# PEER query projection as three fp32r products of high and low halves, with the halves written by the last norm's eviction

## The chip, the cores and the metric

The kernel runs on one core of one Trainium2 chip. The metric is the device time of one execution in microseconds. TensorE is called PE here, VectorE the DVE, ScalarE ACT, GpSimd POOL and the queue that issues most loads SP.

## The reference, cut to what matters

Two transformer blocks run over 512 tokens (four tiles of 128) of width 1024. The change is in the last part of the second block, a layer of experts chosen by product keys (PEER):

```
h2 = rms_norm(x, norm2_g) * (1 + scale2) + shift2
qp = (h @ w_pq).reshape(b, s, 8 heads, 2, 128)          # w_pq is 1024 x 2048
sc = einsum("bshpd,hpnd->bshpn", qp, sub_keys)           # 128 scores for each head and half
s1, i1 = top_k(sc[..., 0, :], 16); s2, i2 = top_k(sc[..., 1, :], 16)
top_s, top_c = top_k(s1[..., :, None] + s2[..., None, :], 16)
expert = e1 * 128 + e2; gate = softmax(top_s)
y = sum over heads and picks of gate * gelu(u[expert] . h) * v[expert]
x = x + gate2 * y
```

## The kernel before

Everything is float32. Large products are done in one of two ways. A plain float32 matmul takes its operands as they are, and shows in the trace as two matmul records. A split product uses fp32r operands: an operand is rounded to a high half, the low half is what is left, and three matmuls (high x high, low x high, high x low, in `passes`) are summed in PSUM.

**Weights** come in 70 chunks of 128 x 2048 through a ring of six buffers. SP loads chunk c once the count `w_used` says that chunk c - 6 is used. The output projection of the second block has chunks 58 to 61, the queries have chunks 62 to 69 (`W_PQ` = 62), each for two of the 16 query blocks. For split chunks the high half is a copy to fp32r by ACT (`high_part`, L693), the low half a subtraction, by the DVE (`low_part`, L1175) or by POOL (`split`, L543 and L545). Before, the query chunks aren't split.

**Output projection and norm.** `mixed_linear` on PE goes over four tiles of tokens and four chunks (L1902). The DVE adds each result to x (L1506, L1509). ACT forms the root mean square of a tile (L626, L629) once that tile's x is complete, the DVE scales the tile (L1060), PE transposes it (L1796), and the DVE's `evac` (L1074, L1076) multiplies by the gain and adds the shift, writing the transposed, normalised tile to hT. On ACT this order is `mix_and_norm`, in which the norm of the last tile comes last.

**Queries and scores.** `queries(c, lo, hi)` (L2131) multiplies block c of w_pq by hT. Blocks 0 and 1 are done on the first three tiles (384 columns) and, when the last tile is through the norm, on its 128 columns. Then h2 of the last tile is transposed back (L2146), and for c = 2 to 16 PE does query block c (512 columns) and the scores of block c - 1 (L2164). ACT copies queries (L959) and scores (L962) out of PSUM.

**Best keys.** For each head the DVE finds the 16 best keys of each half and the 16 best pairs for tiles 0, 1 and 2: `key_tops` and `pair_tops` (L1528 to L1556), 24 units, each head's behind the scores of its two blocks. Between the last units it forms ranks and picks of tile 0 (`tile_ranks`, `tile_keys`, L1573 to L1589). Then 96 chunks of one-hot tables follow (L1645, L1649), which PE multiplies (L2258) into gate tables that are written to memory.

**Experts.** For three tiles all 16384 experts are computed densely; the fourth tile gathers its rows. PE starts with `half_in(s)`, half a key's 128 experts: transposes of u (L2182), the low half of u by a product with the negative identity (L2204), and the split product with h (hd_hi, hd_lo; L2196). 16 of these halves come before the one-hot chunks, the others at fixed places among them. The order is written out by hand on each engine: PE transposes tile 0's picks (`slot_transposes(0)`, L2236) after half 10; ACT takes the exponential of the gates of tile 0 (L981) after half 4, when unit 23 of the DVE is done, and of tiles 1 and 2 after half 14. After 1543 us PE's main loop over 128 keys runs (L2196, L2223).

hd_hi and hd_lo, the halves of h for three tiles, are made by the DVE from hT after the last `evac` (L1517, L1519).

Of the kernel before, what the change touches and what calls it, by code (L numbers as in the profile page):

```python
# [7 lines left out]
ALU = mybir.AluOpType  # L8
# [71 lines left out]
def build(nc, wst, wada, x_in, meta_in, cols_in, rowsa_in, rowsb_in, rope_in, const_in, pos_in,  # L80
          subk_in, peer_u, peer_v, out):
    ctx = ExitStack()
    with ctx:
# [149 lines left out]
        gtmp = cut(r1, 10240, 2, 256)  # L233
        keys = cut(r1, 10720, NKEYS)

        r1_at = big_at + 4 * (WR * CH + 4224 + 17312)
        hd_hi = cut(halves("hd_hi", r1_at + 4 * 4096, KD * DN), 0, KD, DN)
        hd_lo = cut(halves("hd_lo", r1_at + 4 * (4096 + KD * DN), KD * DN), 0, KD, DN)
# [18 lines left out]
        slotT = [gates[:, 0, 0:384], gates[:, 0, 384:768], r1[:, 10240:10624]]  # L257
# [5 lines left out]
        topf = cut(r1, 11104, 2, SLOTS)  # L263
        picks = [v.rearrange("p (a s) -> p a s", a=2) for v in (gates[:, 0, 768:1024], r1[:, 10848:11104], rowsb[:, 0:256])]
# [96 lines left out]
        def high_of(c):  # L361

            if c < W_GU:
                return (mid_hi if c < W_OUT + 2 else w2_hi)[:, (c - W_OUT) % 2, :]
            if c == W_IN2 + 2:
                return w3_hi
            if c < W_LAT:
                return (w_hi if c < W_IN2 else w2_hi)[:, (c - W_GU) % 2, :]
            return (w2_hi if c < W_O2 + 2 else o2_hi)[:, (c - W_O2) % 2, :]
# [161 lines left out]
        def _(pool):  # L531
# [44 lines left out]

            pool.wait_ge(w_used, W_PQ)
            pool.dma_start(subk, subk_in).then_inc(subk_in_s, 16)

# [21 lines left out]
        def _(act):  # L601
# [83 lines left out]
            def high_part(c):  # L685

                chunk(act, c)
                if W_IN2 <= c < W_IN2 + 3:
                    act.wait_ge(a_lo_done, 6)
                    act.wait_ge(w_used, W_IN2 - 2)  # L690
                elif W_GU + 2 <= c < W_LAT:
                    act.wait_ge(w_used, c - 1)
                act.activation(high_of(c), ring[:, c % WR, :], ACT.Copy).then_inc(w_hi_done, 1)  # L693
# [220 lines left out]
            mix_and_norm(T, 3, xn4)  # L914

# [50 lines left out]
            def slots_evac(t):  # L966
                act.wait_ge(slot_tr, t + 1)
                act.activation(slotT[t], ps[:, 2, 0:384], ACT.Copy).then_inc(slot_ready, 1)
# [77 lines left out]
        def _(v):  # L1046
# [4 lines left out]
            def norm(layer, tiles, buf):  # L1051
# [10 lines left out]
                def evac(t):  # L1062
# [9 lines left out]
                    if layer == 3:  # L1072
                        shift = mod[:, 24:24 + KD]
# [502 lines left out]
            def tile_ranks(t):  # L1576

                v.tensor_copy(topf.rearrange("p a s -> p (a s)"), topi[:, t, :])
                pair_ranks(besti[:, t, :], rank_bits, ranks, wrap)
# [59 lines left out]
            for t in range(DT):  # L1639
                v.wait_ge(slot_ready, t + 1)  # L1640
                for c in range(NCH):
# [3 lines left out]
                    v.tensor_tensor(one[n % 4][0], each(keys, CHUNK), over(slotT[t][:, CHUNK * c:CHUNK * c + CHUNK], NKEYS),  # L1645
                                    ALU.is_equal)
                    for k in range(CHUNK):
                        at = CHUNK * c + k
                        mk = v.tensor_scalar(one[n % 4][1][:, k, :], keys, slotT[t][:, P + at:P + at + 1],  # L1649
                                             slotT[t][:, 2 * P + at:2 * P + at + 1], ALU.is_equal, ALU.mult)  # L1650
# [129 lines left out]
        def _(pe):  # L1780
# [364 lines left out]
            for k in range(KD):  # L2145
                mm = pe.transpose(ps[:, 4 + k // 4, P * (k % 4):P * (k % 4) + P], hT[:, k, DT * P:T * P], ident)  # L2146
# [94 lines left out]
            pe.wait_ge(hd_ready, DT)  # L2241
# [118 lines left out]
```

## Time and profile before

| what | value |
|---|---|
| median of 3 runs | 2610.83 us (2608.54 to 2611.42) |
| profiled execution | 2610.15 us, of which the span is 2608.3 us |
| PE busy | 2490.9 us (95%) |
| DVE busy | 1744.4 us (67%) |
| ACT busy | 961.4 us (37%) |
| POOL busy | 376.3 us (14%) |
| mean granted PE clock | 0.989 |

All times of rows are microseconds from the start of the span, mean durations of one instruction are in ns where a row says so. Busy shares are averages over stages with different limits, so that they don't tell what one stage waits for; the views of single stretches do. Matmuls are pipelined: the step from one start to the next is their price, not the length of one record.

### The profile page before, as it was taken

To read this page: it belongs to the slowest core of one execution; us is meant where nothing else is said; L and a number is where in the kernel's file an instruction comes from. 1 tells how busy PE (TensorE), PEld (TensorE's weight loads), DVE (VectorE), ACT (ScalarE), POOL (GpSimd) and SP (SyncE) were. 2 spreads that over 40 slices of the span, in tenths; PEclk is the share of its full clock that TensorE was granted. 3 is DMA by queue.
4 is the path that set the end of the run, shared out by engine and by line. 5 is a ranking of instruction groups with operands and counts; after the bars stand their busy time and mean duration, and the time that the engine had idled before them with its cause. 6 is when DMAs were issued, how large, how long until landed. Compare 5 with 4: busy or idle time off the path is not lost.

```text
span 2608.3 us, 37914 instructions
## 1 busy us (share of the span) xinstructions
PE 2490.9 (95%) x13765; PEld 2137.5 (82%) x13765; DVE 1744.4 (67%) x3801; ACT 961.4 (37%) x1723; POOL 376.3 (14%) x353
## 2 busy tenths in 40 slices
PE   8998889999998989999989999999999999999998
PEld 6777778777778957784688989899899989999987
DVE  5526556553235565548899977887878787877765
ACT  4325532222232645511255653333333333333332
POOL 1000210110000000100000002333333333332300
PEclk9999999999999999999999999999999999999999
DMA  4110005662221220022024567888878887887764
GB/s 187 65 49 1 1 33 192 222 238 99 81 97 66 81 81 1 1 98 73 25 65 170 194 254 275 290 286 284 276 268 282 288 279 268 290 285 259 261 195 153
DMA packets 123511, 431.43 MB, mean 165 GB/s; under 512 B 11696, under 2 KB 36528, under 8 KB 111168
## 3 DMA queue, kind: packets, MB, share of 16 engines
q1 hardware_dynamic: 74768, 241.20, 26.7%
q0 software_dynamic: 47520, 186.14, 20.3%
q8 instruction: 112, 1.84, 0.3%
q10 hardware_dynamic: 1040, 1.67, 0.2%
q14 instruction: 71, 0.58, 0.1%
HBM read 399.61 MB, written 29.36 MB: 164 GB/s over the span
## 4 chain that ended last, share of the span: by engine, by line
PE 75%; DVE 16%; ACT 3%; issue 2%; DVEq 2%; ACTq 1%; DMA 0%
PE ps L2223 19%; PE ps L2196 16%; PE ps L1949 10%; PE ps L1902 7%; PE ps L1806 5%; PE ps L1988 5%; DVE r L1649 4%; PE ps L2182 3%; DVE r L1645 2%; PE ps L2121 1%; PE ps L1871 1%; PE ps L1844 1%; PE ps L2066 1%; ACT r L700 1%; PE ps L2131 1%
## 5 line engine op out<-in xcount | busy, mean ns | idle before, releaser
L2196 PE MATMUL ps<-hd_hi,uT_hi 128*128 128x384 f32 x1024 | 349.9, 342 | 0.8 <-ACT uT_lo L951 0.7
L2196 PE MATMUL ps<-hd_hi,uT_lo 128*128 128x384 f32 x1024 | 346.5, 338 | 0.0
L2196 PE MATMUL ps<-hd_lo,uT_hi 128*128 128x384 f32 x1024 | 346.3, 338 | 0.0
L2223 PE MATMUL ps<-v_hi,ew_hi 128*128 128x512 f32 x768 | 319.5, 416 | 3.7 <-DVE ew_lo L1622 3.1
L2223 PE MATMUL ps<-v_hi,ew_lo 128*128 128x512 f32 x768 | 303.5, 395 | 0.0
L2223 PE MATMUL ps<-v_lo,ew_hi 128*128 128x512 f32 x768 | 301.4, 392 | 0.0
L1602 DVE TENSOR_TENSOR uT_lo<-ps,uT_hi 128x512 fp32r<-128x512 f32 x204 | 140.8, 690 | 144.8 <-ACT uT_hi L924 144.7
L924 ACT ACTIVATE uT_hi<-ps 128x512 fp32r<-128x512 f32 x256 | 152.2, 595 | 189.8 <-PE ps L2182 189.7
L2196 PEld LDWEIGHTS ps<-hd_hi,uT_lo 128*128 128x128 f32 x1024 | 192.6, 188 | 11.0
L2196 PEld LDWEIGHTS ps<-hd_hi,uT_hi 128*128 128x128 f32 x1024 | 192.7, 188 | 9.6 <-ACT uT_lo L951 1.3
L596 POOL DMA_INDIRECT big<-peer_u,r x128 | 144.1, 1126 | 335.3 <-DVE r L1706 311.9
L2196 PEld LDWEIGHTS ps<-hd_lo,uT_hi 128*128 128x128 f32 x1024 | 192.5, 188 | 0.0
L596 POOL DMA_INDIRECT big<-peer_v,r x128 | 143.0, 1117 | 336.3 <-DVE big L1716 326.6
L1607 DVE TENSOR_TENSOR v_lo<-r,v_hi 128x1024 fp32r<-128x1024 f32 x128 | 156.9, 1225 | 38.6 <-ACT v_hi L931 38.6
L1716 DVE SCALAR_TENSOR_TENSOR big<-big,r 128x1024 f32<-128x1024 f32 x128 | 164.5, 1285 | 14.8 <-DMA big<-peer_v,r 2.5
L2223 PEld LDWEIGHTS ps<-v_hi,ew_lo 128*128 128x128 f32 x768 | 144.4, 188 | 32.8
L2223 PEld LDWEIGHTS ps<-v_hi,ew_hi 128*128 128x128 f32 x768 | 144.7, 188 | 29.9 <-DVE v_lo L1607 5.9
L2223 PEld LDWEIGHTS ps<-v_lo,ew_hi 128*128 128x128 f32 x768 | 145.3, 189 | 25.0
L1175 DVE TENSOR_TENSOR w_lo<-big,w_hi 128x2048 fp32r<-128x2048 f32 x42 | 96.0, 2291 | 102.5 <-ACT w_hi L693 102.5
L1706 DVE CUSTOM_DVE_ANT_0 big<-big,r 128x1024 f32<-128x1024 f32 x128 | 155.6, 1218 | 4.0 <-DMA big<-peer_u,r 4.0
L2182 PE MATMUL ps<-const,r 128*128 128x128 f32 x1024 | 153.2, 272 | 3.2 <-DVE uT_lo L1602 3.2
L1806 PE MATMUL ps<-big 128*128 128x256 f32 (+1 forms) x656 | 149.7, 383 | 0.3 <-issue 0.3
(351 smaller groups left out, 5228.5 us busy)
## 6 DMA issues: line engine op xcount, KB each, us to landing
big<-wst SPq DMA_DIRECT2D x70, 1024.0 KB, 4.9
r<-peer_u SPq DMA_DIRECT2D x128, 512.0 KB, 6.9
r<-peer_v SPq DMA_DIRECT2D x128, 512.0 KB, 4.8
r<-wada POOLq DMA_DIRECT2D x48, 512.0 KB, 4.7
gd<-big POOLq DMA_DIRECT2D x24, 1024.0 KB, 8.1
big<-gd SPq DMA_DIRECT2D x32, 768.0 KB, 9.6
x<-x_in SPq DMA_DIRECT2D x4, 512.0 KB, 6.5
xd<-x SPq DMA_DIRECT2D x4, 512.0 KB, 10.2
```

Of the source, the lines that this page charges most:

```text
L596: pool.indirect_dma_start(rows[n % RW], None, table, bass.IndirectOffsetOnAxis(ap=idx[:, n:n + 1], axis=0)).then_inc(got[n % RW], 16)
L924: act.activation(uT_hi[:, s % 2], ps[:, in_bank(s), :].rearrange("p (k n) -> p k n", k=KD // 2), ACT.Copy).then_inc(u_hi_done, 1)
L1602: v.tensor_tensor(uT_lo[:, s % 2], ps[:, in_bank(s), :].rearrange("p (k n) -> p k n", k=KD // 2), uT_hi[:, s % 2].bitcast(F32), ALU.subtra ...
L1607: v.tensor_tensor(v_lo[:, i % VR, :], vraw[:, i % VR, :], v_hi[:, i % 2, :].bitcast(F32), ALU.subtract).then_inc(v_lo_done, 1)
L1706: v.tensor_tensor_reduce(out=urows[n % RW], in0=urows[n % RW], in1=h2, scale=1.0, scalar=0.0, op0=ALU.mult, op1=ALU.add, accum_out=dots[:, ...
L1716: v.scalar_tensor_tensor(out=yacc[:, n % 2, :], in0=vrows[n % RW], scalar=wts[:, n:n + 1], in1=yacc[:, n % 2, :], op0=ALU.mult, op1=ALU.ad ...
L1806: mm = pe.matmul(ps[0:r, bank, 0:w], hT[:, k, t * P:t * P + r], wt[:, k, 0:w], start=(k == 0), stop=(k == KD - 1))
L1902: mm = pe.matmul(ps[:, bank, 0:256], h[:, k, t * P:(t + 1) * P], w[:, k, :], start=(k == 0 and i == 0), stop=(k == KD - 1 and i == 2))
L1949: mm = pe.matmul(ps[:, 2 * (f % 2) + u, lo:hi], w[:, k, u, :], h[:, k, lo:hi], start=(k == 0 and i == 0), stop=(k == KD - 1 and i == 2))
L2182: mm = pe.matmul(ps[:, in_bank(s), P * k:P * k + P], uraw[:, j % UR, at:at + P], ident, is_transpose=True, start=(k == 0 or alone), stop=( ...
L2196: mm = pe.matmul(ps[:, acc_bank(j), 0:DN], w[:, k, :], h[:, KD // 2 * half + k, :], start=(half == 0 and k == 0 and i == 0), stop=(half == ...
L2223: mm = pe.matmul(ps[:, 2 + 2 * t + half, :], w[:, P * t:P * t + P], vv[:, 512 * half:512 * half + 512], start=(i == 0 and n == 0), stop=(i ...
```

## The change

- The four query operands are halves now: w_pq is split, with the high half written by ACT (`high_part`, into two buffers `pq_hi`) and the low half by POOL (`query_low`, into `w_lo`). `queries` does three fp32r matmuls for each of the eight blocks of 128 in place of one float32 matmul. It waits for `w_lo_done`, not for the chunk's load.
- ACT does `high_part` of chunks 62 and 63 after `mix_and_norm`, of 64 to 69 in the loop of the query and score copies, one after every second block.
- POOL issues the load of the sub-keys after the low halves of chunks 62 and 63, and before it did so as its first act in this part.
- `evac` of the last norm writes the sum to a tile of its own (`hq_full`, `h3_full` for the last tile), and then the high half `hq_hi` and the low half `hq_lo`, all on the DVE. The DVE's later split of hT into hd_hi and hd_lo is gone: hd_hi is a part of hq_hi, and hd_lo is a copy of hq_lo that ACT makes at c = 13, when chunk 68 is used.
- Some small tiles move into gaps of hq_hi's buffer (keys, slotT, picks, topf).

```diff
+        hq_hi = cut(halves("hq_hi", r1_at + 4 * 4096, KD * 512), 0, KD, 512)
+        hd_hi = hq_hi[:, :, 0:DN]
+        gaps = cut(r1, 4096, KD, 512)[:, :, DN:512]
+        hq_lo = h_hi[:, :, 0:512]
...
+            def query_low(c):
+
+                if c == W_PQ:
+                    pool.wait_ge(w_lo_done, split_no(W_PQ - 1))
+                pool.wait_ge(w_hi_done, split_no(c))
+                pool.tensor_tensor(w_lo[:, c % WR, :], ring[:, c % WR, :], high_of(c).bitcast(F32),
+                                   ALU.subtract).then_inc(w_lo_done, 1)
+
+            query_low(W_PQ)
+            query_low(W_PQ + 1)
             pool.wait_ge(w_used, W_PQ)
             pool.dma_start(subk, subk_in).then_inc(subk_in_s, 16)
+            for c in range(W_PQ + 2, NCHUNK):
+                query_low(c)
...
-                elif W_GU + 2 <= c < W_LAT:
+                elif W_GU + 2 <= c < W_LAT or c >= W_PQ + 2:
                     act.wait_ge(w_used, c - 1)
+                elif c == W_PQ + 1:
+                    act.wait_ge(mixt_tr, 2 * T)
...
             mix_and_norm(T, 3, xn4)
+            high_part(W_PQ)
+            high_part(W_PQ + 1)
...
+                if c % 2 and W_PQ + c // 2 + 2 < NCHUNK:
+                    high_part(W_PQ + c // 2 + 2)
+                if c == 13:
+                    act.wait_ge(w_used, NCHUNK - 1)
+                    act.wait_ge(ln_hT, 17)
+                    act.activation(hd_lo, hq_lo[:, :, 0:DN], ACT.Copy).then_inc(hd_ready, 1)
...
-                        v.tensor_tensor(dst, src, over(g, n), ALU.mult)
+                        full, high = h3_full if t == T - 1 else hq_full, hq_hi[:, :, at]
+                        v.tensor_tensor(full, src, over(g, n), ALU.mult)
                         v.drain()
-                        v.tensor_tensor(dst, dst, over(shift, n), ALU.add).then_inc(ln_hT, 1)
+                        v.tensor_tensor(full, full, over(shift, n), ALU.add)
+                        v.drain()
+                        v.tensor_copy(high, full)
+                        v.drain()
+                        v.tensor_tensor(hq_lo[:, :, at], full, high.bitcast(F32), ALU.subtract).then_inc(ln_hT, 1)
+                        v.drain()
                         return
...
-            for t in range(DT):
-                full = hT[:, :, t * P:t * P + P]
-                v.tensor_copy(hd_hi[:, :, t * P:t * P + P], full)
-                v.drain()
-                v.tensor_tensor(hd_lo[:, :, t * P:t * P + P], full, hd_hi[:, :, t * P:t * P + P].bitcast(F32),
-                                ALU.subtract).then_inc(hd_ready, 1)
...
-                wt = ring[:, (W_PQ + c // 2) % WR, :].rearrange("p (k n) -> p k n", k=KD)
+                chunk_no = W_PQ + c // 2
+                w_parts = [w.rearrange("p (k n) -> p k n", k=KD)[:, :, P * (c % 2):P * (c % 2) + P]
+                           for w in (high_of(chunk_no), w_lo[:, chunk_no % WR, :])]
                 for k in range(KD):
-                    mm = pe.matmul(ps[:, c % 4, lo:hi], wt[:, k, P * (c % 2):P * (c % 2) + P], hT[:, k, lo:hi],
-                                   start=(k == 0), stop=(k == KD - 1))
+                    for i, (w, h) in enumerate(passes(w_parts, (hq_hi, hq_lo))):
+                        mm = pe.matmul(ps[:, c % 4, lo:hi], w[:, k, :], h[:, k, lo:hi],
+                                       start=(k == 0 and i == 0), stop=(k == KD - 1 and i == 2))
                 return mm
 
-            chunk(pe, W_PQ)
+            pe.wait_ge(w_lo_done, split_no(W_PQ))
             pe.wait_ge(ln_hT, 16)
             queries(0, 0, DN)
...
-                    chunk(pe, W_PQ + c // 2)
+                    pe.wait_ge(w_lo_done, split_no(W_PQ + c // 2))
...
-            pe.wait_ge(hd_ready, DT)
+            pe.wait_ge(hd_ready, 1)
```

## Rows read from the trace of the kernel before

**Rows 1.** Windows, whole core: length, busy time by engine, granted clock, DMA.
```profile
1343.00:1520.00 177.00, 167.16 (x1216) 162.70 (x1215) 175.72 (x496) 95.54 (x164) 11.15 (x20) 0.97 0.43 161
1543.00:2608.00 1065.00, 1054.84 (x5560) 944.83 (x5559) 801.58 (x1266) 369.29 (x587) 283.94 (x253) 1.00 0.77 264
```
**Rows 2.** Waits of the DVE, 1150 to 1600: total, times, longest.
```profile
DVE r L1528 <- ACT r L962: 12.9, 1, 12.9
```
**Rows 3.** Chain that ended last, 1168 to 1186.
```profile
1170.26 6.87 PE ps L2131 x16
1177.12 0.91 PE ps L2164 x8
...
1178.68 0.29 DVE r L1528
```
**Rows 4.** Timeline of the DVE: units 1, 2 and 23.
```profile
1181.86 0.28 DVE L1545 TENSOR_TENSOR r<-r 128x120 f32<-128x120 f32 x1
...
1184.08 0.48 DVE L1528 MAX8 r<-r 128x8 f32<-128x128 f32 x2
...
1303.49 0.22 DVE L1556 TENSOR_SCALAR r<-r 128x16 f32<-128x16 f32 x1
```
**Rows 5.** Timeline of PE around the last norm.
```profile
1151.28 5.40 PE L2131 MATMUL ps<-big 128*128 128x384 f32 x16 [0.26 <-issue]
1156.51 1.04 PE L1796 MATMUL ps<-const,r 128*128 128x128 f32 x8
...
1166.39 1.09 PE L2146 MATMUL ps<-const,big 128*128 128x128 f32 x8
```
**Rows 6.** Timeline of ACT: end of the last norm.
```profile
1153.33 0.29 ACT L629 ACTIVATE lnst<-lnst,eps 128x1 f32<-128x1 f32 x1
```
**Rows 7.** Weight splits by source line: duration ns min/median/max.
```profile
L693 ACT ACTIVATE w_hi<-big x42: 1897/1908/1917, 382.1 to 902.9; 128x2048 fp32r<-128x2048 f32 x42
```
```profile
L545 POOL TENSOR_TENSOR w_lo<-big,w_hi x4: 4517/4524/4532, 320.5 to 1082.5; 128x2048 fp32r<-128x2048 f32 x4
```
**Rows 8.** Timeline of PE: 47 fp32r matmuls of 128 columns, 47 of 512.
```profile
415.56 0.28 PE L1949 MATMUL ps<-h_hi,w_lo 128*128 128x128 f32 x1
...
420.70 0.27 PE L1949 MATMUL ps<-h_lo,w_hi 128*128 128x128 f32 x1
...
432.98 0.39 PE L1949 MATMUL ps<-h_hi,w_lo 128*128 128x512 f32 x1
...
443.60 0.40 PE L1949 MATMUL ps<-h_lo,w_hi 128*128 128x512 f32 x1
```
**Rows 9.** Timeline of the DVE: last eviction and split of h.
```profile
1157.59 1.23 DVE L1074 TENSOR_TENSOR big<-ps,gs 128x1024 f32<-128x1024 f32 x1 [2.94 <-PE ps L1796]
...
1160.03 0.69 DVE L1517 CAST hd_hi<-big 128x1024 fp32r<-128x1024 f32 x1
1160.79 1.23 DVE L1519 TENSOR_TENSOR hd_lo<-big,hd_hi 128x1024 fp32r<-128x1024 f32 x1
```
**Rows 10.** DVE L1202 by source line, and a timeline beside POOL.
```profile
L1202 DVE SCALAR_TENSOR_TENSOR r<-r,coef x16: 767/769/3165, 201.2 to 341.1; 128x528 f32<-128x528 f32 x16
```
```profile
327.37 4.52 POOL L545 TENSOR_TENSOR w_lo<-big,w_hi 128x2048 fp32r<-128x2048 f32 x1
...
329.28 3.17 DVE L1202 SCALAR_TENSOR_TENSOR r<-r,coef 128x528 f32<-128x528 f32 x1
```
**Rows 11.** PE's first matmul after a wait, and the window around it.
```profile
805.65 0.39 PE L1902 MATMUL ps<-w_hi,h_hi 128*128 128x256 f32 x1 [3.87 <-DVE h_lo L1088]
```
```profile
805.00:810.00 5.00, 4.35 (x24) 4.38 (x24) 0.66 0.01 3
```
**Rows 12.** DMA issues, 1100 to 1200: KB each, us to landing.
```profile
r<-subk_in POOLq DMA_DIRECT2D x1, 1024.0 KB, 8.4
```
**Rows 13.** Chain that ended last, 1318 to 1345: halves, then ACT.
```profile
1321.23 1.06 PE ps L2196 x6
...
1333.01 1.28 ACT L981
```

More of the change, by code:

```diff
@@ L232, in build @@
         xn4 = cut(r2, 14336, 2, D)
-        gtmp = cut(r1, 10240, 2, 256)
-        keys = cut(r1, 10720, NKEYS)
+        gtmp = cut(r2, 16384, 2, 256)
         r1_at = big_at + 4 * (WR * CH + 4224 + 17312)
-        hd_hi = cut(halves("hd_hi", r1_at + 4 * 4096, KD * DN), 0, KD, DN)
-        hd_lo = cut(halves("hd_lo", r1_at + 4 * (4096 + KD * DN), KD * DN), 0, KD, DN)
+        hq_hi = cut(halves("hq_hi", r1_at + 4 * 4096, KD * 512), 0, KD, 512)
+        hd_hi = hq_hi[:, :, 0:DN]
+        hd_lo = cut(halves("hd_lo", r1_at + 4 * 8192, KD * DN), 0, KD, DN)
+        gaps = cut(r1, 4096, KD, 512)[:, :, DN:512]
+        keys = gaps[:, 3, :]
+        hq_lo = h_hi[:, :, 0:512]
+        hq_full = cut(r1, 10240, KD, P)
+        h3_full = cut(gates[:, 0, :], 0, KD, P)
+        pq_hi = [cut(halves("pq_hi0", r1_at + 4 * 8192, CH), 0, CH), cut(halves("pq_hi1", r2_at + 4 * 12288, CH), 0, CH)]
         uraw = cut(r2, 9216, UR, D)
@@ L256, in build @@
         one = [[cut(r1, CHUNK * P * (2 * b + a), CHUNK, P) for a in range(2)] for b in range(4)]
-        slotT = [gates[:, 0, 0:384], gates[:, 0, 384:768], r1[:, 10240:10624]]
+        slotT = [cut(gates[:, 0, :], 0, 3, P), cut(gates[:, 0, :], 384, 3, P), gaps[:, 0:3, :]]
         xback = [cut(big, 8192 + D * i, D) for i in range(T)]
@@ L262, in build @@
         wrap = rowsa[:, 0:SLOTS]
-        topf = cut(r1, 11104, 2, SLOTS)
-        picks = [v.rearrange("p (a s) -> p a s", a=2) for v in (gates[:, 0, 768:1024], r1[:, 10848:11104], rowsb[:, 0:256])]
+        topf = gaps[:, 6:8, :]
+        picks = [cut(gates[:, 0, :], 768, 2, P), gaps[:, 4:6, :], cut(rowsb, 0, 2, P)]
         gring = cut(big, 0, 2, 2 * DT, GB * HT)
@@ L366, in high_of @@
                 return w3_hi
+            if c >= W_PQ:
+                return pq_hi[(c - W_PQ) % 2]
             if c < W_LAT:
@@ L964, in _ @@
                                    ACT.Copy).then_inc(sk_ev, 1)
+                if c % 2 and W_PQ + c // 2 + 2 < NCHUNK:
[4 more added lines that the diff above has]
+                    act.activation(hd_lo, hq_lo[:, :, 0:DN], ACT.Copy).then_inc(hd_ready, 1)
             def slots_evac(t):
                 act.wait_ge(slot_tr, t + 1)
-                act.activation(slotT[t], ps[:, 2, 0:384], ACT.Copy).then_inc(slot_ready, 1)
+                act.activation(slotT[t], ps[:, 2, 0:384].rearrange("p (k n) -> p k n", k=3), ACT.Copy).then_inc(slot_ready, 1)
             def half_evac(s):
@@ L1072, in evac @@
                     if layer == 3:
-                        shift = mod[:, 24:24 + KD]
-                        v.tensor_tensor(dst, src, over(g, n), ALU.mult)
+                        shift, at = mod[:, 24:24 + KD], slice(t * P, (t + 1) * P)
+                        full, high = h3_full if t == T - 1 else hq_full, hq_hi[:, :, at]
+                        v.tensor_tensor(full, src, over(g, n), ALU.mult)
                         v.drain()
-                        v.tensor_tensor(dst, dst, over(shift, n), ALU.add).then_inc(ln_hT, 1)
+                        v.tensor_tensor(full, full, over(shift, n), ALU.add)
[4 more added lines that the diff above has]
+                        v.drain()
                         return
@@ L1576, in tile_ranks @@
             def tile_ranks(t):
-                v.tensor_copy(topf.rearrange("p a s -> p (a s)"), topi[:, t, :])
+                v.tensor_copy(topf, topi[:, t, :].rearrange("p (a s) -> p a s", a=2))
                 pair_ranks(besti[:, t, :], rank_bits, ranks, wrap)
@@ L1644, in _ @@
                         v.wait_ge(g_acc, n - 3)
-                    v.tensor_tensor(one[n % 4][0], each(keys, CHUNK), over(slotT[t][:, CHUNK * c:CHUNK * c + CHUNK], NKEYS),
+                    v.tensor_tensor(one[n % 4][0], each(keys, CHUNK), over(slotT[t][:, 0, CHUNK * c:CHUNK * c + CHUNK], NKEYS),
                                     ALU.is_equal)
@@ L1648, in _ @@
                         at = CHUNK * c + k
-                        mk = v.tensor_scalar(one[n % 4][1][:, k, :], keys, slotT[t][:, P + at:P + at + 1],
-                                             slotT[t][:, 2 * P + at:2 * P + at + 1], ALU.is_equal, ALU.mult)
+                        mk = v.tensor_scalar(one[n % 4][1][:, k, :], keys, slotT[t][:, 1, at:at + 1],
+                                             slotT[t][:, 2, at:at + 1], ALU.is_equal, ALU.mult)
                     mk.then_inc(one_ready, 1)
@@ L2145, in _ @@
             for k in range(KD):
-                mm = pe.transpose(ps[:, 4 + k // 4, P * (k % 4):P * (k % 4) + P], hT[:, k, DT * P:T * P], ident)
+                mm = pe.transpose(ps[:, 4 + k // 4, P * (k % 4):P * (k % 4) + P], h3_full[:, k, :], ident)
             mm.then_inc(h2_tr, 1)
```

## Prediction

> **What bounds the kernel now.** I read the windows of busy time first. In 1343 to 1520 us the DVE is busy 175.72 of 177 us, while PE still has gaps; from 1543 us to the end PE is busy 1054.84 of 1065 us [rows 1]. So the end of the run is set by PE from 1543 us on, and the moment at which that last part begins is set by something before it. The waits of the DVE over 1150 to 1600 us say by what: one long wait, 12.9 us, for the second score eviction (ACT L962), and after it only short ones [rows 2]. The chain of waits confirms it: third query product, score product, DVE at 1178.68 [rows 3], and from there DVE instructions one behind another. The DVE does one unit (key_tops and pair_tops of one tile and one head) in 1184.08 - 1178.68 = 5.40 us, and the 23rd ends at 1303.7 us [rows 4], with no wait for PE among them. A head is three units, 16.2 us, and on PE two query products and two score products: 2 x (6.87 + 0.91) = 15.6 us [rows 3] and some 0.5 us for drains, just less. Then come the DVE's ranks and one-hot tables to 1543 us. The reader should see that between 1179 and 1543 us PE's time costs nothing by itself; the start of the DVE's first unit and whatever stops the DVE count one for one.
>
> **What the change does to the start of the first unit.** Before, query product 0 starts at 1151.28 us, right behind the output projection [rows 5]. Now it waits for the low half of weight chunk 62. That is POOL's subtraction behind ACT's rounded copy, and in ACT's order the copy stands behind the norm of tile 3, whose last instruction ends at 1153.33 + 0.29 = 1153.62 us [rows 6]. The copy takes 1.91 us and POOL's subtraction 4.52 [rows 7]: 1153.62 + 1.91 + 4.52 + 0.05 = 1160.1 us. Late by **8.8 us**. The two other conditions of that product are met earlier: the eviction of tile 2 grows by a cast and a subtraction, 0.76 + 1.23 = 2 us [rows 9], but it lies inside the projection of tile 3, where the DVE waits for PE; without that idle time each of its 2 us would count.
>
> Prices of the new products, from rows of the same shape: 512 columns, 46 steps in 443.60 - 432.98 us, 0.231 us each, so 24 take 5.54; 128 columns, 46 steps in 420.70 - 415.56, 0.112 each [rows 8]; 384 columns, six in 1.06 us, 0.176 each, so 24 take 4.2 [rows 13].
>
> Query 0 on three tiles took 1156.51 - 1151.28 = 5.23 us; now 4.2 at full clock. But PE has stood 9 us. After a wait of 3.87 us at 805.65 us the granted clock was 0.66 over the next 5 us, that is 1.2 GHz for about 3.4 us and then 2.4 [rows 11]; 3.4 us at the lower level give back half, 1.5 to 1.7. Net **+0.5**.
>
> From the transposes of tile 3 (1156.51) to those of h2 (1166.39) were 9.88 us [rows 5]. Now the eviction starts 1.08 us after the first transpose (1157.59 against 1156.51) and is a product, a sum, a cast and a subtraction: 2.44 + 0.10 for a drain + 0.76 + 1.23 = 4.5 us [rows 9], so it ends 5.6 us after the first transpose, when PE is done with query 1 (0.9 + 4.2) and has waited half a us. Then the last tile's share of queries 0 and 1, 48 products at 0.112: 5.4 us. Together 11.1, **+1.2**. (At 128 columns three passes cost more than the old two.) From the h2 transposes to query 2 nothing changes. Query 2 itself: 5.54 for 6.87, **-1.3**.
>
> The sub-key load, which POOL now issues behind two subtractions (near 1164.7 us), lands in 8.4 us [rows 12], by 1173.2; PE asks for it at about 1178. Hidden by 5 us; each us beyond that would count. The loads of weight chunks follow the used counts and are early too. The first unit starts 8.8 + 0.5 + 1.2 - 1.3 = **9.2 us** later, near 1187.9 us.
>
> **What is gained and not seen.** Thirteen further query products save 1.33 us each, 17 us of PE. PE then needs about 13.4 us a head (2 x (5.54 + 0.91) + 0.5) where the DVE needs 16.2, and it reaches the expert part 17.3 - 9.2 = 8 us earlier than before, at about 1186 + 13 x 6.7 + 2 = 1275. There it runs until ACT stops at the gate exponential of tile 0, which waits for the DVE's 23rd unit. The DVE loses the split of hd (six instructions, 5.8 us), but it did these before 1166 us, right ahead of its long wait [rows 2, 9]: worth nothing. ACT's six further copies of 1.91 us and the 3072-element copy of the low halves (about 2.8 us by the length of the 2048-element one) lie between its copies: per query block of at least 5.5 us it has only two short ones to do.
>
> **What POOL does to the DVE.** Six more subtractions of 4.52 us run on POOL (chunks 64 to 69). The first ends about when unit 1 starts; five fall into the units. Each unit has, 3.18 us from its start, a tensor_tensor with both inputs in SBUF (L1545) [rows 4]. The nearest row is the attention's scalar_tensor_tensor (L1202), also with two SBUF inputs: 0.77 us alone, but 3.17 us when it started inside a POOL subtraction, ending at 332.45, 0.56 us after POOL's end at 331.89 [rows 10]. The DVE stood until POOL was through. So a POOL subtraction that covers L1545 stops the DVE for its remainder. POOL follows the query pace of 13.4 us: after release the DVE passes one L1545 at 5.40, before the next subtraction begins (13.4 - 4.5 = 8.9), and meets it with the next at 10.8, 1.9 us into it: 2.6 us lost, and the pattern repeats itself. Only the first of the five, whose phase is open, can cost anything between 0 and 4.5. I take 2.5 for each of the five, **12.6 us**, by the row of L1202. Bounds: 0 (L1545 isn't held) and 5 x 4.52 = 22.6. Between them lies a shared port that only slows both: L1202 grew to 3.17 / 0.77, four times its length; four times 0.28 us is 0.85 us more, five times, 4 us. Against that stands that L1202 ended so close behind POOL.
>
> The Trainium skill, "SBUF — State Buffer", section "SBUF: two separate sides", calls what the two engines share "an exclusive lock, not a bandwidth split", held for a whole instruction by the one that starts first. By that rule the term is 12.6 us, by a split it would be the 4; the trace agrees with the rule where it can be seen, L1202 ending 0.56 us behind POOL's 4.52 us instruction.
>
> **The restart.** A half takes (1333.0 - 1321.2) / 4 = 2.9 us [rows 13]. PE does six by about 1293 and then stands until unit 23 ends, at 1303.7 + 9.2 + 12.6 = 1325.5: some 30 us, and its clock falls as in [rows 11]. The halves behind it run at 1.2 GHz for 3.4 us, and the chain from the slot transposes to the exponentials of tiles 1 and 2 runs through PE (the halves, then ACT at 1333.01) [rows 13]. Part of the 1.7 us lies in waits for ACT: I take **0.5 us**, bounds 0 and 1.7.
>
> **Sum.** 9.2 + 12.6 + 0.5 = 22.3 us on the DVE's chain. What follows is shifted as a whole, since PE's halves are at fixed places among the one-hot chunks. The profiled execution took 2610.15 us (span 2608.3 and 1.85 around it), which makes 2632.5; the median is 0.7 us higher. I say **2633 us**.
>
> **Rivals.**
> 1. POOL doesn't hold the DVE, or by a split only: 2610.8 + 9.7 = 2620.5, with the split 2625. For it: L1545 is short, 120 elements, and no row shows such a one beside POOL. Against it: L1202. Chance 0.17.
> 2. Every subtraction costs the DVE nearly its whole length, because more of the unit's instructions are held or the phases fall badly, and the restart costs 1.7: 9.2 + 22.6 + 1.7 = 33.5, 2644. The unit's other instructions have one input in SBUF or a few elements, which speaks against. Chance 0.12.
> 3. Faster: the DVE's units follow the scores, and PE's gain reaches the end: 9.2 - 17.3 = -8.1, 2603. It takes a unit under 13.4 / 3 = 4.5 us; it is 5.40 [rows 4]. Chance 0.04.
> 4. No effect: the low half of chunk 62 is ready in time and POOL harmless. ACT's order forbids it. Chance 0.03.
>
> My forecast has 0.64: its own range is 2626 to 2640. The range of 8 in 10 takes in rival 1's lower value and reaches towards rival 2: 2619 to 2641. About 5 us (0.2%) is what measurement tells from no change. Faster 0.04, same 0.03, slower 0.93.
>
> **What would show it.** PE should stand about 9 us before the first query product, waiting for POOL's w_lo, with a fall of the granted clock behind it. DVE L1528 should first start at 1187 to 1189. Query products should take 5.5 us, PE should stand some 30 us in the expert part's halves. L1545 should show a maximum of 2 to 5 us, five or so times, each ending with a POOL subtraction; if all are 0.28, rival 1 holds. I'd be wrong in kind if the first DVE unit started before 1180, or if the units waited for scores.

## The result and the profile after

| | before | after |
|---|---|---|
| median of 4 runs, us | 2610.24 | 2635.7 |
| lowest and highest, us | 2608.54 to 2611.42 | 2632.94 to 2637.85 |
| profiled execution, us | 2610.15 | 2632.94 |
| span, us | 2608.3 | 2631.1 |
| mean granted clock | 0.989 | 0.982 |

The changed kernel is slower: the ratio is 1.0097, with an interval of 1.0085 to 1.0109, or 25.5 us between the medians.

The windows of busy time, in the columns of [rows 1], show the same two parts as before, both 23 us later. Windows of the same lengths hold nearly the same instructions and busy times as in [rows 1], so nearly the whole difference was made ahead of 1366 us.

```profile
1366.00:1543.00 177.00, 165.05 (x1217) 159.92 (x1216) 175.74 (x495) 95.17 (x163) 11.29 (x20) 0.99 0.43 161
1566.00:2631.00 1065.00, 1055.91 (x5560) 946.10 (x5560) 801.98 (x1267) 369.91 (x589) 285.63 (x253) 1.00 0.77 264
```

Two waits of PE between 1145 and 1560 us (total, times, longest) are new: one for POOL's low half in front of the first query product, and one for ACT in the expert part's halves, where before PE waited 0.7 us for the same tile.

```profile
PE ps L2229 <- ACT uT_lo L975: 32.6, 2, 32.0
...
PE ps L2164 <- POOL w_lo L590: 9.1, 1, 9.1
```

How the first of them comes about is seen in the timelines of ACT, POOL and PE. The lines answer to [rows 5, 6, 7].

```profile
1151.67 0.30 ACT L649 ACTIVATE lnst<-lnst,eps 128x1 f32<-128x1 f32 x1
1151.87 3.69 ACT L715 ACTIVATE pq_hi<-big 128x2048 fp32r<-128x2048 f32 x2
```
```profile
1153.91 9.01 POOL L590 TENSOR_TENSOR w_lo<-big,pq_hi 128x2048 fp32r<-128x2048 f32 x2 [68.54 <-ACT pq_hi L715]
```
```profile
1149.08 0.28 PE L1932 MATMUL ps<-h_lo,mid 128*128 128x256 f32 x1
1158.47 0.69 PE L2164 MATMUL ps<-hq_hi,pq_hi 128*128 128x384 f32 x1 [9.10 <-POOL w_lo L590]
...
1164.54 1.03 PE L1826 MATMUL ps<-const,r 128*128 128x128 f32 x8
```

The projection's last product starts at 1149.08 us; ACT is through with the norm only at 1151.97, the first copy and the first subtraction (4.51 of the 9.01 us) follow, and the product starts at 1158.47. Moments of one trace can't be set against those of another here: already before the change's first instruction this trace runs 1.66 us ahead of the one of before, whose last product of the projection starts at 1150.74. So I compare lengths inside each trace, by this chain of waits, which answers to [rows 3]:

```profile
1158.47 6.23 PE ps L2164 x24
...
1170.26 5.58 PE ps L2164 x48
1175.83 0.11 issue
1175.94 1.10 PE ps L2179 x8
...
1179.81 5.51 PE ps L2164 x24
...
1186.88 0.29 DVE r L1558
```

From the projection's last product to the first instruction of the DVE's first unit it is 1186.88 - 1149.08 = 37.80 us, where before it was 1178.68 - 1150.74 = 27.94: 9.9 us more.

In the units, some DVE records are unusually long. Here is one beside POOL, in the timelines:

```profile
1209.01 4.61 POOL L590 TENSOR_TENSOR w_lo<-big,pq_hi 128x2048 fp32r<-128x2048 f32 x1 [8.78 <-ACT pq_hi L715]
```
```profile
1209.08 0.30 DVE L1578 MAX8 r<-r 128x8 f32<-128x136 f32 x1
1209.45 0.09 DVE L1580 MATCH_VALUE_LOAD r<-r 128x8 f32 x1
1209.53 0.29 DVE L1580 FIND_INDEX8 r<-r 128x8 uint32<-128x136 f32 x1
1209.74 0.07 DVE L1581 MATCH_VALUE_LOAD r<-r 128x8 f32 x1
1209.80 0.28 DVE L1581 MATCH_REPLACE8 r<-r 128x136 f32<-128x136 f32 x1
...
1210.82 2.83 DVE L1586 TENSOR_SCALAR r<-r 128x16 f32<-128x16 f32 x1
```

Eight DVE instructions, five of which are shown, run inside POOL's at their usual length. Then the TENSOR_SCALAR over 16 elements a partition takes 2.83 us in place of 0.22, and ends at 1213.65, with POOL's end at 1213.62. Five records of the units are so long: L1586 at 1197.55 (2.70), 1210.82 (2.83) and 1224.22 (2.76), L1574 at 1235.67 (4.68) and 1250.90 (2.75). Beyond the usual 0.22 that is 14.6 us. By source line (duration ns min/median/max), over the whole run:

```profile
L1574 DVE TENSOR_SCALAR r<-r x32: 227/234/4681, 1189.9 to 2243.9; 128x16 f32<-128x16 f32 x32
```
```profile
L1575 DVE TENSOR_TENSOR r<-r x32: 271/276/278, 1190.1 to 2244.0; 128x120 f32<-128x120 f32 x32
```

L1575 is the tensor_tensor with two SBUF inputs, the L1545 of [rows 4]. It was never held here.

The 23 units run from 1186.88 to the gate exponential of tile 0 at 1326.50: 139.6 us, where before it was 1303.83 - 1178.68 = 125.15. From there to the slot transposes of tile 0 it is 17.73 us, before 16.85, by these rows of PE and ACT, first of after, then of before:

```profile
1344.23 0.38 PE L2269 MATMUL ps<-const,gates 128*128 128x128 f32 x2
```
```profile
1326.50 0.40 ACT L1011 ACTIVATE r<-r,zero 128x128 f32<-128x128 f32 x1 [31.87 <-DVE r L1586]
```
```profile
1320.68 0.44 PE L2236 MATMUL ps<-const,gates 128*128 128x128 f32 x2 [0.42 <-DVEq L1589]
```
```profile
1303.83 0.40 ACT L981 ACTIVATE r<-r,zero 128x128 f32<-128x128 f32 x1
```

The three lengths add up to 9.9 + 14.5 + 0.9 = 25.2 us, beside 25.5 between the medians. The profiled executions differ by 22.8: the one of after is the lowest of its four, ran 1.66 us ahead in the part that the change doesn't touch, and took 0.75 us less from the slot transposes to the end (1286.87 for 1287.62).

### The profile page after: what moved, and what is told of

The parts are those of the page before. It is cut to its first block, busy times and chain, and to the rows that moved or that the text cites. A ratio compares the mean times of both kernels' runs of the same rounds, so it can differ in the third digit from the quotient of the medians.

```text
span 2631.1 us, 38239 instructions
## 1 busy us (share of the span) xinstructions
PE 2475.1 (94%) x13909; PEld 2165.0 (82%) x13909; DVE 1760.9 (67%) x3803; ACT 977.8 (37%) x1732; POOL 414.5 (16%) x361
## 4 chain that ended last, share of the span: by engine, by line
PE 75%; DVE 16%; ACT 3%; issue 2%; DVEq 2%; ACTq 1%; DMA 0%; POOL 0%; POOLq 0%
PE ps L2256 19%; PE ps L2229 16%; PE ps L1979 10%; PE ps L1932 7%; PE ps L1836 5%; PE ps L2018 5%; DVE r L1679 4%; PE ps L2215 3%; DVE r L1675 2%; PE ps L2151 2%; PE ps L1901 1%; PE ps L1874 1%; PE ps L2096 1%; ACT r L722 1%; DVE r L1238 1%
## 5 line engine op out<-in xcount | busy, mean ns | idle before, releaser
L2229 PE MATMUL ps<-hq_hi,uT_hi 128*128 128x384 f32 x1024 | 350.9, 343 | 32.6 <-ACT uT_lo L975 32.6
L2229 PE MATMUL ps<-hq_hi,uT_lo 128*128 128x384 f32 x1024 | 347.5, 339 | 0.0
L2229 PEld LDWEIGHTS ps<-hq_hi,uT_hi 128*128 128x128 f32 x1024 | 193.5, 189 | 41.4 <-ACT uT_lo L975 33.2
L2229 PEld LDWEIGHTS ps<-hq_hi,uT_lo 128*128 128x128 f32 x1024 | 193.3, 189 | 11.0
L1932 PE MATMUL ps<-w_lo,h_hi 128*128 128x256 f32 x528 | 148.8, 282 | 0.0
```

Source lines behind the costliest of these rows:

```text
L1932: mm = pe.matmul(ps[:, bank, 0:256], h[:, k, t * P:(t + 1) * P], w[:, k, :], start=(k == 0 and i == 0), stop=(k == KD - 1 and i == 2))
L2229: mm = pe.matmul(ps[:, acc_bank(j), 0:DN], w[:, k, :], h[:, KD // 2 * half + k, :], start=(half == 0 and k == 0 and i == 0), stop=(half == ...
```

## The experiments

All were timed beside the kernel before, whose median was 2610.65, 2610.2 and 2611.15 us beside the three groups of them (e1 to e4; e5, e6, e7, e9; e8 and e10). Gains are counted from the changed kernel's 2635.7 us. Three lengths are read from each trace, of which there is one a kernel: **start** (the projection's last product to the first MAX8 of the units), **units** (from there to the first gate exponential) and **slots** (from there to the first slot transpose).

| kernel | median, us | ratio to before, interval | start | units | slots |
|---|---|---|---|---|---|
| before | | | 27.94 | 125.15 | 16.85 |
| after | 2635.7 | 1.0097 [1.0085, 1.0109] | 37.80 | 139.62 | 17.73 |
| e1_no_low | 2618.54 | 1.0031 [1.0019, 1.0042] | 38.13 | 125.00 | 16.95 |
| e2_early | 2629.8 | 1.0071 [1.0057, 1.0085] | 27.18 | 139.63 | 17.85 |
| e3_pieces | 2625.43 | 1.0050 [1.0036, 1.0064] | 38.71 | 128.77 | 16.94 |
| e4_early_pieces | 2618.32 | 1.0031 [1.0022, 1.0041] | 28.80 | 128.72 | 16.98 |
| e5_dve_low | 2634.31 | 1.0086 [1.0072, 1.0099] | 38.68 | 136.23 | 18.20 |
| e6_swap | 2634.26 (one run) | | 37.94 | 139.82 | 17.74 |
| e7_warm | 2634.49 | 1.0093 [1.0078, 1.0107] | 37.80 | 139.67 | 17.67 |
| e8_all_pieces | 2613.89 | 1.0015 [1.0006, 1.0024] | 27.17 | 128.82 | 17.44 |
| e9_all | 2613.23 | 1.0010 [1.0001, 1.0019] | 27.20 | 128.74 | 16.93 |
| e10_two_chunks | 2609.34 | 0.9999 [0.9989, 1.0008] | 27.21 | 125.04 | 16.94 |

**e1_no_low: is it POOL's work that stretches the units?** The low halves of chunks 64 to 69 are left out; the second product of these takes the high half again.

```
-                query_low(c)
+                pool.wait_ge(w_hi_done, split_no(c))
+                pool.drain().then_inc(w_lo_done, 1)
...
-                           for w in (high_of(chunk_no), w_lo[:, chunk_no % WR, :])]
+                           for w in (high_of(chunk_no), w_lo[:, chunk_no % WR, :] if c < 4 else high_of(chunk_no))]
```

> The low halves of weight chunks 64 to 69 are left out: POOL forms none, and the second of the three query products takes the high half again, so that PE does as many products as in the changed kernel. Everything else is as changed. If POOL's subtractions hold the DVE's units (the trace of the changed kernel shows five TENSOR_SCALARs of 2.70, 2.83, 2.76, 4.68 and 2.75 us in place of 0.22), they fall to 0.22 and 14.6 us go: 2635.7 - 14.6 = 2621, or 10 to 11 us above the kernel before. Rival: the long records are only how the trace books a wait that the DVE would have anyway (for scores, or for PE); then the DVE waits elsewhere and the time stays at 2633 to 2637. Third: the whole loss is the late start; then also no change.

The units went back to 125.0 us, and no record of these lines is long, as by source line for L1575 of this kernel (its TENSOR_SCALAR over 16 elements):

```profile
L1575 DVE TENSOR_SCALAR r<-r x32: 225/234/288, 1190.2 to 2228.4; 128x16 f32<-128x16 f32 x32
```

17.2 us of the medians are gone, with as many PE products and the same ACT copies; 14.6 were expected. In the traces the units give back 14.6 us and the slots 0.8, and the profiled executions differ by 15.6; the rest of the 17.2 is no more than the runs of one kernel differ by. So the stretch of the units is POOL's, whole.

**e2_early: the other half, the late low half of chunk 62.** ACT copies the high halves of chunks 62 and 63 ahead of the norm of tile 2's sums, so that POOL makes the low halves during the projection.

```
+                    if t == T - 1 and first:
+                        high_part(W_PQ)
+                        high_part(W_PQ + 1)
...
-            high_part(W_PQ)
-            high_part(W_PQ + 1)
```

> The high halves of chunks 62 and 63 are made by ACT before the norms of tiles 2 and 3, so that POOL has both low halves when the output projection ends. The first query product should start within 0.5 us of its end, without a fall of the clock, and the DVE's first unit comes 9.9 us earlier than in the changed kernel, perhaps one more, since three passes over 384 and 512 columns are shorter. If the late start costs one for one, the time is 2635.7 - 10 to 11 = 2625 to 2626. Rival: POOL's two subtractions now lie beside the DVE's residual sums and evictions and hold them, so that PE waits in the projection instead; then up to 9 us of it come back and the time stays above 2630.

The first query product no longer waits, the start is 10.6 us shorter, but the median fell by 5.9 us only, where 10 to 11 were expected. The rest was lost again ahead of the start, in the norm of tile 2. Timelines of POOL, DVE and PE:

```profile
1130.57 9.35 POOL L590 TENSOR_TENSOR w_lo<-big,pq_hi 128x2048 fp32r<-128x2048 f32 x2 [42.48 <-ACT pq_hi L715]
```
```profile
1132.18 3.29 DVE L1546 TENSOR_TENSOR x<-x,r 128x256 f32<-128x256 f32 x1
1135.38 1.21 DVE L1106 TENSOR_TENSOR r<-ps,gs 128x1024 f32<-128x1024 f32 x1
1136.67 4.33 DVE L1108 TENSOR_TENSOR r<-r,mod 128x1024 f32<-128x1024 f32 x1
```
```profile
1147.64 1.97 PE L1827 MATMUL ps<-const,r 128*128 128x128 f32 x8 [3.20 <-DVE r L1091]
```

Two DVE instructions with both inputs in SBUF were held by the two subtractions (3.29 for 0.42 us and 4.33 for 1.23); the one between them, which reads a PSUM input, was not, though POOL was at work: 1.21. The norm's result came late, PE waited 3.2 us and went on at the lower clock (0.50 from 1147.6 to 1152 us): from the transposes to the projection's last product it is 1157.19 - 1147.64 = 9.55 us, in the changed kernel 1149.08 - 1142.08 = 7.0. That is 3.2 + 2.55 = 5.75 us lost for 10.6 won, 4.9 by these lengths beside 5.9 between the medians, and explains why not 10 us were gained. In the units one of the five long records now lies on the tensor_tensor with two SBUF inputs (at 1233.28, 4.69 us).

**e3_pieces: does the DVE wait for one POOL instruction, or for POOL's work?** The subtractions of chunks 64 to 69 are cut into eight instructions of 256 columns.

```
+                for j in range(8 if c >= W_PQ + 2 else 1):
+                    n = CH // 8 if c >= W_PQ + 2 else CH
+                    at = slice(n * j, n * j + n)
+                    low = pool.tensor_tensor(w_lo[:, c % WR, at], ring[:, c % WR, at], high_of(c)[:, at].bitcast(F32),
+                                             ALU.subtract)
+                low.then_inc(w_lo_done, 1)
```

> POOL's subtractions of chunks 64 to 69 are done in eight instructions of 256 columns each, the same elements in all. If POOL holds the DVE for the length of one instruction, a hold is at most some 0.7 us in place of 2.7 to 4.7; there may be two or three short ones where there was one long one, 1 us for each of five chunks: 14.6 falls to about 5 and the time to 2626. If instead what counts is the data that POOL moves (a shared bandwidth, the same elements), nothing changes: 2633 to 2637.

POOL now works longer, 5.60 us a chunk for 4.60, and yet the DVE loses 3.6 us in place of 14.5. Had POOL's busy time been what counts, it would have lost more. In the timelines of POOL and DVE:

```profile
1202.57 5.59 POOL L593 TENSOR_TENSOR w_lo<-big,pq_hi 128x256 fp32r<-128x256 f32 x8 [7.73 <-ACT pq_hi L719]
```
```profile
1207.66 0.53 DVE L1578 TENSOR_SCALAR r<-r 128x16 f32<-128x16 f32 x1
```

There are nine held instructions now in place of five. They take 0.53 to 0.88 us, never more than one piece (5.6 / 8 = 0.7 us) beyond their own length. What holds the DVE is the one POOL instruction in progress, for its remainder.

**e4_early_pieces: do the two parts add?** Both edits together.

> Both edits together: early high halves of chunks 62 and 63, and subtractions in eight pieces. If the two costs are independent terms of one chain, the gains add: 2635.7 - 10.5 - 9.6 = 2615.6, 5 us above the kernel before, of which about 5 are the short holds and 1 the colder restart. If both edits remove the same wait, it stays near 2625.

The gains are 5.9 and 10.3 us alone and 17.4 together: they add within the intervals. The 3.24 us wait for tile 2's norm is still there, since chunks 62 and 63 were not cut.

**e5_dve_low: the DVE makes the low halves itself.** One subtraction ahead of each of heads 0 to 5; POOL keeps chunks 62 and 63.

```
-            for c in range(W_PQ + 2, NCHUNK):
-                query_low(c)
...
+                if h == 0:
+                    v.wait_ge(w_lo_done, split_no(W_PQ + 1))
+                if W_PQ + h + 2 < NCHUNK:
+                    low_part(W_PQ + h + 2)
```

> The low halves of chunks 64 to 69 are made by the DVE itself, one ahead of each of heads 0 to 5, and POOL keeps only chunks 62 and 63. If the 14.6 us are POOL holding the DVE, no long record of L1574 or L1586 is left, and in their place stand six subtractions of 2.3 to 2.5 us on the DVE: 14 to 15 us, so the time stays at 2634 to 2636 us. Rival, that the units are longer for another reason (the eviction's new layout, ACT's writes): the long records stay and the six subtractions come on top, 2649 to 2651 us.

No record of the units is held, and the six subtractions take 2.29 us each, the first in the DVE's wait for the scores, five in the units, which are 11.1 us longer than before (14 to 15 were expected, with all six counted). The start and the slots are 0.9 and 0.5 us longer than in the changed kernel. The DVE's own work for these halves costs nearly what waiting for POOL's costs: 2634.31.

**e6_swap: which instruction is held?** In pair_tops the tensor_tensor of 128x120 comes ahead of the tensor_scalar of 128x16.

```
-                v.tensor_scalar(c0[:, 0:16], topv[:, 1, :], topv[:, 0, 0:1], None, ALU.add)
...
+                v.tensor_scalar(c0[:, 0:16], topv[:, 1, :], topv[:, 0, 0:1], None, ALU.add)
```

> In pair_tops the two instructions that build the candidates change places: first the tensor_tensor of 128x120, then the tensor_scalar of 128x16. Theory: POOL's instruction stops the first DVE instruction of a kind that can be stopped, whichever it is, while MAX8, FIND_INDEX8 and MATCH_REPLACE8 pass. Then at least one long record moves to the tensor_tensor with two SBUF inputs, the total beyond the normal lengths stays between 12 and 17 us, and the time stays within 3 us of 2635.7. Rival: only the tensor_scalar is stopped; then the tensor_tensor never exceeds 0.3 us and all long records stay on the two tensor_scalar lines.

There are five long records again, 14.7 us beyond the usual lengths. One of them has moved to the tensor_tensor (at 1252.84, 3.01 us); at 1237.90 the tensor_scalar behind it took 4.58. So both forms are held, and the one that comes first while POOL is at work is held.

**e7_warm: is the 0.9 us of the slots the clock's?** 280 transposes into a bank that nothing reads stand ahead of half 6.

```
+                if s == 6:
+                    for n in range(280):
+                        pe.transpose(ps[:, 5, 0:P], ident, ident)
```

> 280 transposes of 128x128 into a bank that nothing reads stand ahead of half 6, where PE stands 32 us in the changed kernel. Theory: the lower clock behind the wait costs the chain from the 23rd unit to the slot transposes 0.9 us; with PE busy this stretch is 17.0 us long in place of 17.9 and the time 2634.8 us, unless the transposes outlast the wait, which would show as a later half 6 and be longer by what they overrun. Rival: the clock's share lies in waits for ACT, and the stretch stays at 17.9.

The slots stayed at 17.67 us. The windows of this kernel show why (busy PE, PEld, DVE, ACT, POOL, granted clock, DMA):

```profile
1290.00:1327.00 37.00, 36.17 (x315) 35.77 (x313) 32.63 (x184) 3.56 (x7) 0.00 (x0) 1.00 0.10 30
1327.00:1332.00 5.00, 3.37 (x12) 2.95 (x13) 4.63 (x9) 3.47 (x6) 0.00 (x0) 0.76 0.01 3
1332.00:1337.00 5.00, 5.00 (x30) 4.83 (x29) 4.78 (x6) 2.27 (x4) 0.00 (x0) 0.89 0.00 0
```

The clock was at 1.00 up to the exponential at 1326.64, and fell at some 1329.6 us, behind two waits of PE for ACT (1.40 and 1.05 us). It came back no sooner than in the changed kernel. So the transposes had not kept the lower clock off the stretch, and the experiment doesn't show what a stretch at full clock would be worth there. e10_two_chunks, below, shows that: there PE doesn't stand, the clock never falls at this place, and the slots take 16.94 us, beside 16.85 in the kernel before. A window of e10:

```profile
1302.00:1318.00 16.00, 14.44 (x85) 13.49 (x85) 15.26 (x16) 9.11 (x16) 0.00 (x0) 1.00 0.30 98
```

Other kernels show what the lower clock costs: e8_all_pieces and e4_early_pieces both stood 21 us at this place and needed 17.44 and 16.98 us.

```profile
1306.00:1311.00 5.00, 4.91 (x14) 4.21 (x15) 4.70 (x6) 2.89 (x4) 0.00 (x0) 0.50 0.00 0
```
```profile
1314.00:1319.00 5.00, 4.90 (x18) 4.27 (x19) 4.70 (x6) 2.92 (x4) 0.00 (x0) 0.60 0.00 0
```

The first is e8, the second e4, each from 1 us behind the exponential on: in e4 the clock came back within the five us, in e8 just behind them. What orders the kernels is the moment at which the clock is back, counted from the exponential and read from windows of 1 us. With its slots, that is 4.4 and 16.95 us in e1, 4.6 and 16.93 in e9, 4.9 and 16.98 in e4, 5.9 and 17.44 in e8, 6.4 and 17.67 in e7, 6.5 and 17.73 in the changed kernel, 6.8 and 17.85 in e2, 7.5 and 18.20 in e5. A return within 4.9 us costs nothing beside e10, and each us later costs some 0.46. So 0.8 of the 0.9 us are the price of the lower clock. Why it comes back 4 us after PE's restart in e4 and 6.6 us after it in e5 stays open; e5, with the shortest standing (7 us), had the longest return.

**e8_all_pieces and e9_all: all eight low halves in pieces, early.** e8 is e4 with chunks 62 and 63 cut as well; e9 has 170 of the transposes of e7 on top.

> High halves of chunks 62 and 63 ahead of the norm of tile 2 (as e2_early), all eight low halves on POOL in pieces of 256 columns, and 170 transposes ahead of half 6. In e2_early the two whole subtractions stopped two DVE instructions of tile 2's norm and made PE wait 3.2 us in the projection; with pieces that wait should be under 1 us and the first query some 3 us earlier. From e4_early_pieces at 2618.3: minus 3 to 4 for that and minus 0.9 for the clock gives 2613.5 to 2614.5 us. Rival, that POOL's early work only moves the cost (the pieces together delay the norm as much): 2617.5. The kernel before, 2610.6, is reached by neither, since 3.8 us of holds in the units and the dearer products of 128 columns are left.

> e9_all without the 170 transposes: high halves of chunks 62 and 63 ahead of the norm of tile 2, all eight low halves on POOL in pieces of 256 columns. In e9_all the clock fell all the same once PE waited for ACT behind the release, and the stretch from the first gate exponential to the slot transposes was 16.93 us, in e4_early_pieces, with 21 us of standing, 16.9 too. So the transposes do nothing and the time is that of e9_all, 2613 us. Rival, that they were worth the 0.9 us that the changed kernel shows: 2614 us or more, and 17.7 us for the stretch.

The wait for tile 2's norm is gone in e8 (PE stands 0.26 us ahead of its transposes, for 3.24 in e4), and the start is 27.17 us, shorter than before by 0.8. The median of e8 is 4.4 us below e4's: most of what e2 had lost to the two held instructions is back. e9 and e8 are equal within their intervals, so the medians can't tell what the transposes bring. By the two traces the slots are 0.5 us longer without them. The expectation for e8 had 16.9 us for this stretch and its rival 17.7; the 17.44 us lie between, and so the experiment decides for neither.

In e8 a cast on the DVE was held as well, 1.07 us for its usual 0.69, with POOL's pieces running from 1127.93 to 1142.74:

```profile
1132.86 1.07 DVE L1114 CAST hq_hi<-r 128x1024 fp32r<-128x1024 f32 x1
```

**e10_two_chunks: only queries 0 to 3 in three passes.** Queries 4 to 15 are fp32 products from the loaded chunk, on the high half of the norm's output, whose low part is left out for them. ACT and POOL make no halves of chunks 64 to 69.

```
+                if c >= 4:
+                    wt = ring[:, chunk_no % WR, :].rearrange("p (k n) -> p k n", k=KD)
+                    for k in range(KD):
+                        mm = pe.matmul(ps[:, c % 4, lo:hi], wt[:, k, P * (c % 2):P * (c % 2) + P],
+                                       hq_hi[:, k, lo:hi].bitcast(F32),
+                                       start=(k == 0), stop=(k == KD - 1))
+                    return mm
```

> Three passes for queries 0 to 3 alone (chunks 62 and 63, highs ahead of the norm of tile 2, lows in pieces); queries 4 to 15 are fp32 products again, straight from the loaded chunk. They take the high half of the norm's output as their fp32 input, so its low part is left out for them; instructions and their times are those of whole fp32 products. Theory: the rest of the distance between e9_all and the kernel before, 3 us, is the holding of the DVE in the units (3.7 us), and the start of the units is level with before. Then the 23 units take 125 us, PE stands little at half 6, and the time is 2609 to 2610.5 us, the same as the kernel before. Rival, that the cost lies in the start or in the longer work of ACT and POOL elsewhere: 2613 us with units of 125 us.

The units are 125.04 us and the time is that of the kernel before, 0.9999. Against e8, the 3.7 us of holding are gone and 0.5 us of the slots, and nothing is left. This version isn't faster than the kernel before by anything that could be measured, and as a whole kernel it would need room for the full output of the norm beside its halves.

## Why the prediction came out as it did

- **What bounds the kernel, and the gain that isn't seen.** Right. In e10 twelve of the sixteen queries went back to the dearer form, against e8, and the run became 4.5 us shorter. PE reached the half after s=5 early and stood there 32.0 us (some 30 expected).
- **Start of the first unit, 9.2 us.** Measured 9.9. Wait for POOL: (1158.47 - 1149.08) - (1151.28 - 1150.74) = 8.85 for 8.8. Query 0 in the lower clock: 6.07 us to the transposes for 5.23 before, +0.8 for +0.5, as the clock was back only some 3.9 us after the restart (0.56 over 1158 to 1163 us), where I took 3.4 over from [rows 11]. From the transposes to those of h2: 1175.94 - 1164.54 = 11.4 for 9.88, +1.5 for +1.2. Query 2: 5.51 for 6.87, as said. Two sizes are off by 0.3 us, the mechanism is right, and e2_early shows it by taking the wait away.
- **POOL holds the DVE, 12.6 us.** Right in kind, wrong in the instruction, and near in size partly by luck. Measured 14.6. The text named L1545, since it has two SBUF inputs; held were the tensor_scalars over 16 elements, with one input. By the prediction's own sign (if all of L1545 stay at 0.28 us, there is no hold) the trace would have spoken for rival 1, since L1575 was never held; the sign was tied to the wrong instruction. The moment 1.9 us into POOL's instruction, worked out for L1545, is where L1586 starts at three of the five meetings and L1574 at the last: what recurs once a unit comes at the same distance after a release, whichever instruction it is. But L1574 and L1575 come earlier in the unit, and at the three meetings they started only 0.2 to 0.4 us ahead of POOL and just passed. At the fourth L1574 started together with POOL: 4.45 us in place of 2.5. Had the phases lain 0.4 us otherwise, the other three could have cost as much as the fourth, some 6 us more; that is an estimate, 3 x (4.45 - 2.5), and no run shows it. The term was sized as five times 2.5; it is four times 2.5 and once 4.45. e1, e3 and e5 show the cause, e2 and e6 that the other form can be held as well. What the text says against rival 2, that the unit's other instructions have one input or a few elements, was no reason: the held ones have one tensor input and 16 elements.
- **The restart, 0.5 us.** Measured 0.9, inside its bounds. The lower clock lasted 5.6 us from PE's restart, not 3.4. e7 didn't take it away; over the kernels the term varies between 0.1 and 1.35 us with the moment at which the clock comes back.
- **The sum.** 22.3 us predicted, 25.2 measured: 0.7 + 1.9 + 0.4 more. The median lies 2.7 us above the 2633, inside the forecast's own range.
- **The rivals.** Rival 1 (no hold) falls with the five records, its split as well: an instruction of 0.22 us that takes 4.68 isn't sharing. Rival 2 (nearly the full length each time) came true once in five, and its reason, that more of the unit's instructions are held, for L1574 and L1586. Rival 3 falls: in e1, where PE is as fast and nothing is held, a unit still takes 5.4 us. Rival 4 falls with the 9.1 us wait.

On the page: the Trainium skill, "SBUF — State Buffer", section "SBUF: two separate sides", has a lock that the starting instruction keeps to its end. The trace agrees (2.83 us, ending 0.03 us behind POOL), and e3 with its pieces tells it from a split. The same page's section "Who interferes with whom" names two kinds of DVE instruction that can meet that lock: copy, cast and tensor_scalar when they run in a two-port mode, and a tensor_tensor with both inputs in SBUF. The runs agree as far as they go: L1574 and L1586 are tensor_scalars, and so of the first kind if they run in such a mode, which no trace here shows; the cast of e8 is of that kind too. The records at 1233.28 in e2 and 1252.84 in e6 are of the second, and the tensor_tensor with a PSUM input, outside both, took its usual 1.21 us in e2. By the first kind the prediction should have counted L1586's forerunner L1556 [rows 4] and L1574's; I had read the form with two inputs alone. No run here measures a copy from SBUF beside POOL.

## What to carry to other kernels

A faster product on an engine that isn't the bound is paid for by whatever makes its operands: look first at who rounds and subtracts, whether that is ready when the first product could start, and whom it stops meanwhile. If POOL must work beside a DVE on the critical path, cut its instructions short: eight pieces cost POOL 1 us more a chunk and gave the DVE 11 us back in six chunks. Estimate such holding as meetings times the remainder of POOL's instruction at each, over all DVE instructions of the forms that are seen to be held, even if they are as small as 16 elements a partition. The phase of those that lie near POOL's start decides between the remainder and the full length, so give the estimate both bounds.

## What the runs showed of the hardware

- A DVE TENSOR_SCALAR over 16 elements a partition (0.22 us) took up to 4.68 us beside one POOL TENSOR_TENSOR of 2048 columns (4.60 us). MAX8, FIND_INDEX8 and MATCH_REPLACE8 passed at their usual length (0.30, 0.29 and 0.28 us) inside the POOL instruction at 1209.01, and so did a TENSOR_TENSOR with a PSUM input (1.21 us in e2).
- Not every TENSOR_SCALAR is held. In the attention part of the changed kernel, inside POOL's subtractions of 128x2048, those that read PSUM (128x64 and 128x128) kept their usual 0.28 and 0.34 us, those over one element a partition their 0.15 and 0.27, and a COPY from PSUM (128x128) its 0.29.

```profile
1074.38 4.53 POOL L553 TENSOR_TENSOR w_lo<-big,w_hi 128x2048 fp32r<-128x2048 f32 x1
```
```profile
1076.02 0.15 DVE L1518 TENSOR_SCALAR sst<-sst 128x1 f32<-128x1 f32 x1
1076.71 0.28 DVE L1528 TENSOR_SCALAR r<-ps,sst 128x64 f32<-128x64 f32 x1 [0.46 <-PE ps L2151]
```

- The record of L1574 at 1235.67 begins 0.04 us ahead of POOL's at 1235.71, and yet it was held to POOL's end, at 1240.32:

```profile
1235.67 4.68 DVE L1574 TENSOR_SCALAR r<-r 128x16 f32<-128x16 f32 x1
1240.26 0.27 DVE L1575 TENSOR_TENSOR r<-r 128x120 f32<-128x120 f32 x1
```

So when two records begin 0.04 us apart, their order doesn't tell which engine has the lock.
- PE's clock stood at 1.00 through 31 us of transposes and still fell some 3.5 us behind them, after PE had waited twice for ACT (e7). After the changed kernel's 32 us of standing it was at 0.50, which is 1.2 GHz, for 5.6 us from the restart, in e5 after 7 us of standing for 6.6.
